# Second block's experts: two slabs loaded ahead instead of four, x kept in SBUF, the last norm taken into the pass by tiles

## What is computed

```python
xf = _rms_norm(h, norm_ffn_w[l]) * (1.0 + scale_f) + shift_f
h = h + gate_f * _hierarchical_moe(xf, w_group[l], b_group[l], w_router[l], b_router[l], w_gate[l], w_up[l], w_down[l])
...
return _rms_norm(h, norm_out_w)
```

## Time and profile before

| | us |
|---|---|
| median of three runs | 3667.17 |
| profiled execution | 3666.75 |
| span of its instructions | 3664.9 |
| TensorE busy in the span | 3198.9 (87%) |
| VectorE busy | 1487.8 (41%) |
| ScalarE busy | 989.3 (27%) |
| GpSimd busy | 46.5 (1%) |

### The profile page before, as it was taken

One profiled execution on the slowest core, in us unless ns is written; L12 is line 12 of the kernel. 1 busy time (PEld: TensorE's weight loads), 2 busy tenths in 40 slices (PEclk: granted clock), 3 DMA queues, 4 the chain that ended last, 5 costly groups with the idle time before them and its releaser, 6 DMA issues. The chain is left out here.

```text
span 3664.9 us, 54483 instructions
## 1 busy us (share of the span) xinstructions
PE 3198.9 (87%) x23420; PEld 1778.7 (49%) x23420; DVE 1487.8 (41%) x3058; ACT 989.3 (27%) x1956; POOL 46.5 (1%) x65
## 2 busy tenths in 40 slices
PE   7889998899889999879995978887989899884996
PEld 3566666666765555444443323334455454541332
DVE  2666667766645685630004101002333424332122
ACT  2343433434313555620002000003224232310001
POOL 0000000000000000000000000000000000000000
PEclk9999999999879999889997999998999999986998
DMA  4122221122231222251135999982301111027998
GB/s 172 52 66 64 65 82 59 61 64 63 64 104 49 69 83 84 84 170 67 60 130 232 421 421 421 421 359 104 118 36 72 46 72 46 0 109 312 413 417 330
DMA packets 119456, 555.31 MB, mean 152 GB/s; under 512 B 32320, under 2 KB 35120, under 8 KB 83632
## 3 DMA queue, kind: packets, MB, share of 16 engines
q1 hardware_dynamic: 113072, 532.95, 38.0%
q0 software_dynamic: 3456, 12.58, 0.9%
q10 hardware_dynamic: 2688, 6.29, 0.4%
HBM read 518.03 MB, written 33.74 MB: 151 GB/s over the span
## 5 line engine op out<-in xcount | busy, mean ns | idle before, releaser
L2332 PE MATMUL mh_ps<-mh_w_ahead,xmT 128*128 128x512 f32 x768 | 336.5, 593 | 0.0
L2067 PE MATMUL ex_ps<-ex_ring,ex_xs 128*64 128x512 f32 x896 | 247.3, 643 | 51.1 <-DMA ex_ring<-expert_slabs_in 43.9
L493 PE MATMUL rw_ps<-hT,rw_w 128*128 128x512 f32 (+1 forms) x640 | 259.0, 535 | 6.1 <-PEq L63 5.8
L2332 PEld LDWEIGHTS mh_ps<-mh_w_ahead,xmT 128*128 128x128 f32 x768 | 144.7, 190 | 167.2 <-issue 165.2
L2067 PEld LDWEIGHTS ex_ps<-ex_ring,ex_xs 128*64 128x64 f32 x896 | 82.6, 148 | 205.6 <-issue 205.6
L1258 PE MATMUL sg_ps<-hTp,sg_w 128*128 128x512 f32 x384 | 170.3, 597 | 0.0
L493 PEld LDWEIGHTS rw_ps<-hT,rw_w 128*128 128x128 f32 x640 | 113.0, 192 | 89.7 <-issue 80.0
L2316 PE MATMUL mh_ps<-xmT,mh_w_ahead 128*128 128x512 f32 x256 | 125.2, 623 | 14.9 <-PEq L63 8.6
L2151 DVE TENSOR_TENSOR ex_hid<-ex_hid,ex_ps 128x512 f32<-128x512 f32 x16 | 11.0, 688 | 288.7 <-PE ex_ps L2067 288.7
L1782 PE MATMUL se_ps<-se_w,se_mT 128*128 128x512 f32 x256 | 113.6, 601 | 8.0 <-DMA se_w<-w_out_in 8.0
L1258 PEld LDWEIGHTS sg_ps<-hTp,sg_w 128*128 128x128 f32 x384 | 73.8, 193 | 91.0 <-issue 90.9
(11 more groups left out here) (602 smaller groups left out, 5349.9 us busy)
## 6 DMA issues: line engine op xcount, KB each, us to landing
ex_ring<-expert_slabs_in SPq DMA_DIRECT2D x148, 1024.0 KB, 26.9
ge_ring<-expert_slabs_in SPq DMA_DIRECT2D x52, 2048.0 KB, 11.7
mh_w_ahead<-head_slabs_in SPq DMA_DIRECT2D x16, 2048.0 KB, 7.9
rw_mod_w<-mod_w_in SPq DMA_DIRECT2D x64, 384.0 KB, 4.0
ex_first<-expert_slabs_in SPq DMA_DIRECT2D x22, 1024.0 KB, 26.3
rw_mod_w<-ada_in SPq DMA_DIRECT2D x64, 256.0 KB, 3.3
sg_kern<-cum_dram SPq DMA_DIRECT2D x64, 256.0 KB, 3.3
ex_ring<-expert_slabs_in SPq DMA_DIRECT2D x7, 2048.0 KB, 13.6
```

Source lines behind the costliest of these rows:

```text
L493: mm = pe.matmul(where[j, part], w[:, k, P * j:P * j + P], tokens, start=k == 0, stop=k == KC - 1)
L2067: mm = pe.matmul(ps[halves[j], bank, :], src[:, k, halves[j]], home(g + j)[0][:, k, :], start=k == 0, stop=k == KC - 1)
L2332: mm = pe.matmul(ps[:, 4 + t, :], xmT[:, k, P * t:P * t + P], w[:, slot, k, :], start=k == 0, stop=k == KC - 1)
```

## The change

1. `settle` takes `x_keep` and, in its third use, `x_out=None`: the sum stays in the SBUF tensor x4, the four stores to x3 are not made. The loads of gate, orow and gate_q are issued at the end of this stage's load list, and counted by a semaphore `landed.rows` that `route` waits for.
2. `route` loads two slabs ahead instead of four, and no x and no rows.
3. In `grouped_experts` SP loads slabs 2 to 5 of pair 0 behind the first rows and quarters. TensorE starts pair 0 after the turn of rows alone; the turn of quarters comes after the first rows product, and both quarter products of pair 0 come after the second rows product.
4. After pair 7 only slabs 0 and 1 of pair 0 are loaded again instead of 0 to 3. Of the last four quarter stores two are issued by SP.
5. `last_residual` is gone: in the pass, each tile's mean, root, reciprocal and product follow its adds, and SP stores it. The products are written to the memory of ge_xs and ge_xsq. A Sqrt of one column is issued ahead of the first tile.

```diff
-                for t in range(NTT):
+                for t in range(NTT if x_out is not None else 0):
                     sp.wait_ge(s.summed, H * t + H)
                     sp.dma_start(x_out[tile(t), :], x[:, t, :]).then_inc(s.x_stored, 16)
...
-        with stage(nc) as (s, block, _):
+        landed, rows = before
+        with stage(nc, landed.all) as (s, block, _):
             @block.sync
             def _(sp):
                 for dst, src in ahead:
                     sp.dma_start(dst, src).then_inc(s.ahead_in, 16)
+                sp.wait_ge(landed.rows, rows)
                 sp.wait_ge(s.ahead_in, 16 * len(ahead))
...
+        normed = lambda t: (xs, xsq)[t // 2][:, t % 2, :, :].rearrange("p k n -> p (k n)")
...
                     load_rows(0)
                     load_quarters(0)
-                    load_slab(0, 4)
-                    load_slab(0, 5)
+                    for n in range(2, 6):
+                        load_slab(0, n)
                     load_rows(1)
-                    for i in range(NP):
-                        nxt = (i + 1) % NP
-                        if 1 <= i and i + 1 < NP:
+                    for i in range(NP - 1):
+                        if i:
                             load_rows(i + 1)
-                        if i % 2 == 1 and i + 1 < NP:
+                        if i % 2 == 1:
                             load_quarters((i + 1) // 2)
                         for n in range(4):
                             sp.wait_ge(s.up_used, 2 * i + n // 2 + 1)
-                            load_slab(nxt, n)
-                        if i + 1 < NP:
-                            sp.wait_ge(s.down_used, i + 1)
-                            load_slab(nxt, 4)
-                            load_slab(nxt, 5)
-                    for n in range(6):
+                            load_slab(i + 1, n)
+                        sp.wait_ge(s.down_used, i + 1)
+                        load_slab(i + 1, 4)
+                        load_slab(i + 1, 5)
+                    sp.wait_ge(s.up_used, 2 * NP - 1)
+                    load_slab(0, 0)
+                    load_slab(0, 1)
+                    sp.wait_ge(s.yeq_kept, NP)
+                    for h in range(2):
+                        sp.dma_start(quarter_rows(NP - 1, 1, h), yeq[quarter[2 + h], :]).then_inc(s.yeq_out, 16)
+                    for t in range(NTT):
+                        sp.wait_ge(s.normed, t + 1)
+                        sp.dma_start(x_out[tile(t), :], normed(t)).then_inc(s.x_stored, 16)
+                    sp.wait_ge(s.x_stored, 16 * NTT)
+                    for n in range(2):
                         sp.wait_ge(slab_in[n], 16 * NP)
...
                     turn_rows(0)
-                    turn_quarters(0)
                     for i in range(NP):
                         last = i + 1 == NP
-                        pe.wait_ge(s.xs_kept, turns_before(i + 1, i // 2 + 1))
+                        pe.wait_ge(s.xs_kept, turns_before(i + 1, i // 2 + 1) if i else 1)
                         for n in range(2):
                             for b in range(2):
-                                if i:
-                                    pe.wait_ge(slab_in[2 * n + b], 16 * i)
+                                if n:
+                                    pe.wait_ge(slab_in[2 + b], 16 * i + 16)
+                                elif i:
+                                    pe.wait_ge(slab_in[b], 16 * i)
...
-                            up_quarters(i, n)
+                            if i:
+                                up_quarters(i, n)
+                            elif n == 0:
+                                turn_quarters(0)
+                        if i == 0:
+                            pe.wait_ge(s.xs_kept, 2)
+                            up_quarters(0, 0)
+                            up_quarters(0, 1)
...
-                        for b in range(2):
+                        for b in range(2 if i + 1 < NP else 1):
                             for h in range(2):
...
+                    act.activation(sq[:, 0:1], cst("ones")[:, 0:1], ACT.Sqrt).then_inc(s.squared, 1)
                     for t in range(NTT):
                         act.wait_ge(s.added, t + 1)
-                        if t:
-                            act.wait_ge(s.squared, t)
+                        act.wait_ge(s.squared, t + 1)
                         act.activation(sq[:, :], x[:, t, :], ACT.Square, accum_out=ss[:, t:t + 1]).then_inc(s.squared, 1)
+                        act.wait_ge(s.mean, t + 1)
+                        act.activation(ss[:, t:t + 1], ss[:, t:t + 1], ACT.Sqrt).then_inc(s.root, 1)
...
+                    def scale(t):
+                        dve.wait_ge(s.root, t + 1)
+                        link(dve.reciprocal(ss[:, t:t + 1], ss[:, t:t + 1]))
+                        dve.scalar_tensor_tensor(normed(t), x[:, t, :], ss[:, t:t + 1], orow, ALU.mult, ALU.mult).then_inc(s.normed, 1)
...
                         ins.then_inc(s.added, 1)
+                        if t:
+                            scale(t - 1)
+                        dve.wait_ge(s.squared, t + 2)
+                        dve.tensor_scalar(ss[:, t:t + 1], ss[:, t:t + 1], 1.0 / D, EPS, ALU.mult, ALU.add).then_inc(s.mean, 1)
+                    scale(NTT - 1)
```

More of the change, by code:

```diff
@@ L1958, in _ @@
                 dve.tensor_copy(lg.rearrange("p t n -> p (t n)"), ps[:, 6, 0:NL * NTT])
-def last_residual(nc, ss, orow, x, x_out):
-    NTT = SEQ // P
-    with stage(nc) as (s, block, _):
-        @block.sync
-        def _(sp):
-            for t in range(NTT):
-                sp.wait_ge(s.normed, t + 1)
-                sp.dma_start(x_out[P * t:P * t + P, :], x[:, t, :]).then_inc(s.x_stored, 16)
-            sp.wait_ge(s.x_stored, 16 * NTT)
-        @block.scalar
-        def _(act):
-            act.wait_ge(s.mean, 1)
-            act.activation(ss, ss, ACT.Sqrt).then_inc(s.root, 1)
-        @block.vector
-        def _(dve):
-            link = linker(dve, s.dve_link)
-            dve.tensor_scalar(ss, ss, 1.0 / D, EPS, ALU.mult, ALU.add).then_inc(s.mean, 1)
-            dve.wait_ge(s.root, 1)
-            link(dve.reciprocal(ss, ss))
-            for t in range(NTT):
-                dve.scalar_tensor_tensor(x[:, t, :], x[:, t, :], ss[:, t:t + 1], orow, ALU.mult, ALU.mult).then_inc(s.normed, 1)
 CAP = 2 * SEQ // NE
@@ L2752, in first_of_ties, with route @@
         link(dve.tensor_tensor(hot[:, :, e], hot[:, :, e], a, ALU.is_gt))
-def route(nc, cst, raw, bias, weight, slot, npass, ahead):
+def route(nc, cst, raw, bias, weight, slot, npass, ahead, before):
     NTT, G, E = SEQ // P, 4, 4
@@ L3296, in program @@
                 mixer_heads(nc, masks, xmT, tok, a["head_slabs"], a["gdn_taps"], a["ret_decay"], rope, norm_w[:, :], m, w, xe_dram[0:NE * SLOTS, :])
-            settle(nc, cst, (m, a["w_out2"], None, None), (mod2[0:1, 2 * D:3 * D], None), (col_a, col_sh), x2, x3,
-                   (a["norm_ffn"], part(mod2, 0, 4), part(mod2, 0, 3)), (a["route_w"], 20), wide(20), xn_keep=xn)
+            gate_of = lambda lo, hi, n: mod2[0:1, 5 * D + lo:5 * D + hi].broadcast_to([n, hi - lo])
+            rows = [nc.sbuf_tensor(name, shape, F32, side="right") for name, shape in (("x4", [P, 4, D]), ("gate4", [P, D]), ("gate_q", [P, 512]), ("orow4", [P, D]))]
+            x, gate, gate_q, orow = (keep.enter_context(r) for r in rows)
+            landed = Sems(nc, keep)
+            settle(nc, cst, (m, a["w_out2"], None, None), (mod2[0:1, 2 * D:3 * D], None), (col_a, col_sh), x2, None,
+                   (a["norm_ffn"], part(mod2, 0, 4), part(mod2, 0, 3)), (a["route_w"], 20), wide(20), xn_keep=xn, x_keep=x,
+                   ahead=[(gate[:, :], gate_of(0, D, P), landed.rows), (orow[:, :], a["norm_out"].broadcast_to([P, D]), landed.rows)] +
+                         [(gate_q[32 * n:32 * n + 32, :], gate_of(512 * (n % 2), 512 * (n % 2) + 512, 32), landed.rows) for n in range(4)])
         with ExitStack() as moe:
             sb = lambda name, shape: moe.enter_context(nc.sbuf_tensor(name, shape, F32))
-            x, gate, gate_q, orow, ss = sb("x4", [P, 4, D]), sb("gate4", [P, D]), sb("gate_q", [P, 512]), sb("orow4", [P, D]), sb("ss4", [P, 4])
+            ss = sb("ss4", [P, 4])
             ye_dram = scratch("ye_dram", (NE * SLOTS, D))
@@ L3305, in program @@
             npass = moe.enter_context(nc.sbuf_tensor("npass", [P, 1], mybir.dt.int32))
[L3306 to L3310 removed]
+            route(nc, cst, wide(20), route_b, weight[:, :, :], slot[:, :, :, :], npass[:, :], [(ring[:, n, :], a["expert2_slabs"][n]) for n in range(2)],
+                  (landed, 96))
             grouped_experts(nc, cst, slot[:, :, :, :], weight[:, :, :], npass, (col_a, col_sh), xn, (xe_dram, ye_dram), a["expert2_slabs"], ring,
[L3312 to L3313 removed]
+                            (gate[:, :], gate_q[:, :]), x, ss, orow[:, :], out)
 def kernel(**inputs):
```

24 lines of the change are left out of this document (10 added, 14 removed).

## The result

The changed kernel takes 3643.93 us (3640.17 to 3645.55, four runs) where the kernel before takes 3667.43 beside it (four runs): ratio 0.9935, 95% interval 0.9918 to 0.9952, so 23.5 us faster. The forecast was 3643.6. The profiled execution took 3643.77 us.

A forecast was written before the change was run, and what follows sets the result against it. Routing was taken as bound by its loads, pairs by TensorE with transfers close behind, the tail by vector work and small transfers. Gains 17.5 + 0 + 0 + 3.1 + 0 + 3.0 = 23.6 us gave 3643.6 us, range 3640.5 to 3646 (0.72).

The forecast's parts named there:

- Part 1: Route stage: without two slab loads, x and six row loads, VectorE is late next; gain 17.5 us, bounds 17.0 to 18.0.
- Rival (c): Route stage: the second slab lands as late as the third did, 3.3 us less gain, 3646.9 us; chance 0.04.
- Parts 2 and 3: Row loads moved into settling, x stores dropped: 0, at most 0.5 us lost; scatter with the same eight indirect DMAs: 0.
- Part 4: First pair: first product ahead of the turn of quarters, less clock loss; gain 3.1 us, bounds 1.2 to 3.7.
- Part 5: Steady pairs: refills shift, lead of the next pair's rows shrinks 3.5 us to 1.7; no loss, bounds 0 to 3 us.
- Rival (a): Pairs 1 to 3: lead gone, TensorE waits for rows or slabs, 3 to 6 us together, 3646.6 to 3649.6; chance 0.14.
- no reserve in rate: Steady pairs: each moves 14.15 MB in 34.0 us, 416 GB/s against 417 shown, so transfers have reserve only in lead.
- Rival (d): Seven refilled pairs: transfers set the pace, 4.4 us more each at 368 GB/s, kernel 7.3 us slower; chance 0.02.
- Part 6: End of the pass: split quarter stores 1.3 us, norm stage gone 1.7 us; gain 3.0 us, bounds 1.2 to 4.3.
- two take 1.4 us, so the gathers start 1.3 us earlier: End of the pass: ScalarE issues two quarter stores instead of four, which took 2.77 us; gain 1.3 us.
- The Sqrt table load: End of the pass: put where ScalarE idles 23.76 us, cost 0; coming back at each tile, 5.1 us in all.
- Rival (b): Tail: GpSimd's gathers and VectorE's operations delay each other; two operations per gather cost about 4 us, 3647.6; chance 0.04.

The follow-up runs named there:

- four_ahead: Changed kernel with routing loading four slabs ahead again, and four reloaded at the end of the pass; x and rows stay out of routing: 3653.17 us.
- x_back: Changed kernel with x stored to memory again by the second settling stage and loaded back in routing behind its two slabs: 3645.27 us.
- after_again: The changed kernel run once more without an edit, for its scatter: 3641.52 us, ratio to the kernel before 0.9923.
- warm_34: Changed kernel plus 34 unused 128x512 products on TensorE ahead of pair 0's turn of rows: 3655.27 us.
- quarters_first: Changed kernel with the turn of quarters made before pair 0's first product again, loads unchanged: 3643.97 us, ratio to the kernel before 0.9931.
- stores_on_act: Changed kernel with all four last quarter stores issued by ScalarE again, still two slabs reloaded: 3641.74 us.
- wrap4: Changed kernel with slabs 0 to 3 of pair 0 reloaded after pair 7 instead of 0 and 1, stores still split: 3642.82 us.
- traffic_1mb: Changed kernel plus one unread 1 MB load per pair in pairs 1 to 6: 3651.00 us.
- traffic_half: Changed kernel plus one unread 0.5 MB load per pair in pairs 1 to 6: 3649.72 us.

## Why the prediction was right, and where its steps were not

**Part 1, route: right.** 17.5 forecast, 17.56 measured; ge_row 17.23 us after the logits where 17.3 was worked out (3310.7 less 3293.39). The reading that SP's wait for the last load held the stage, and that VectorE is next, is shown by four_ahead and x_back. Rival (c) is out: the second slab landed 1.7 us ahead of VectorE's last write, the third load would have been 3.9 us too late (21.08 against 17.2).

**Parts 2 and 3: right,** at nothing. The six row loads were issued from 3235.07 to 3237.84 in the settling stage, which took 80.31 us against 81.12. In the stretch from 3240 to 3260 the DMA share fell from 0.13 to 0.02: what I had read there was the first x store (issued at 3243.39). And the scatter took 15.98 us against 15.97.

**Part 4, first pair: right within its bounds, by up to 0.5 us too high.** 3.1 forecast; 2.60 measured in the first profile, 3.05 in the second. The order is worth 3.9 us where I had 3.6. The clock took more than I allowed: the first product ran 2.60 us over its warm time in after (2.16 in after_again) against 1.34 in before. That is a loss of 0.8 to 1.3 us where the term was 0.5. Out of the bounds of 1.35 to 2.2 for the whole loss I had taken 1.85; it was 2.16 and 2.60. The slabs came in time, as worked out.

**Part 5, pairs: right in the sum, near the edge.** No loss, 245.80 us in both. The lead did shrink, by 4.8 us and not by 3.5: pair 2's rows were issued at 3375.05 and landed 20.2 us later, at 3395.25. The two rows, landing and use:

```profile
DMA to landing us min/median/max: 20.2/20.2/20.2
...
3395.64 1.04 PE L2937 MATMUL ge_ps<-consts,ge_xg 128*128 128x128 f32 x8
```

So 0.4 us were left where I had 1.7; in eight other profiles with this order it is 0.2 to 0.4 (1.0 in warm_34, where pair 0 began 13 us later behind the same loads). Rival (a) missed by no more than that: that nothing stalled was partly luck. quarters_first, with the old order, has 4.5 us there, so it is the later release of the first slabs that spends the lead. What I had wrong is "no reserve in rate": with a limit of 425 against a demand of 416 GB/s a lag shrinks, and the lead grows again, 1.2 us for pair 3 (3409.41 plus 19.5, wanted at 3430.14), 2.2 for pair 4 and 3.2 for pair 7 (3545.40 plus 17.5, wanted at 3566.12). Rival (d) needed 368 GB/s; the transfers carry 425. The 377 GB/s of the earlier trace rows, its one row in favour, has a DMA share of 0.95 beside it and holds the moment between the second refill and the third, as the prediction's part 5 had said itself. The figure of the Trainium skill that I had set beside it, about 358 GB/s for a core ("DMA: Bandwidth & Descriptors", section "Specifications"), is the rate of a memory stack shared out over two cores; here one core runs, and this loop shows 417 to 426.

**Part 6, tail: too low, by 1.6 us.** 3.0 forecast, 4.64 measured (2.07 - 0.27 + 3.13 - 0.29) in the first profile, a little beyond the bound of 4.3. Two terms were off.
- The step "two take 1.4 us, so the gathers start 1.3 us earlier" gave the split a gain of 1.3. It measured 0.3 to 0.7. The gain ahead of the gathers was 2.07 because of the two slabs that are no longer loaded again, to which I had given nothing: I had asked only what is queued on SP's queue, not how long a small store takes among transfers of others. The sum was nearer than its reason.
- The norm was put at 1.7 and is worth 2.9 to 3.3. The working had 19.85 us from the first add to the last product's end, and it takes 18.42. Three tiles take 0.30 us less each for reciprocal, product and mean (1.46 against 6.1/4 + 0.23 = 1.76), and the last tile's handoff takes 0.53 us from the end of the product ahead (3634.95 + 1.29) to the start of the last one, at 3636.77, where 0.75 stood beside a mean and a reciprocal of their own: 0.7 less. Against that the late row took 0.81 us and not 0.4. I had added busy times of small operations that overlap their neighbours.

The Sqrt table load was hidden, as worked out (3612.76, behind the last quarter stores), and did not come back. Rival (b) has its mechanism and no price that shows, instead of 4 us. Its reading that the earlier trace rows shows a third of the lock (0.44 us) was wrong: a gather waits for the whole rest of the add, which was partly over when the gather began.

**The sum.** By seams the change is worth 24.8 us in the first profile, 1.2 more than forecast. The scatter ahead of the logits took 1.9 of it back, and the time outside of the span was 1.67 us instead of 1.85. The median's 0.3 us of difference to the forecast is closer than the steps deserve: their errors were +0.1, -0.5 and +1.6 us, and the total of one kernel moves by more than these (3641.52 us in the second set). So the closeness is luck; the parts' sum, 24.8 against 23.6, is the fair measure. Why the stretch ahead of the third settling stage varies by up to 12 us between profiles was not looked into.

## What to carry to other kernels

A stage that preloads for the next one ends with its last load: count the bytes in the queue, keep what is needed first, and let the rest ride behind the first consumer; here each 2 MB past the second slab cost some 4 us. Where transfers and TensorE run at the same pace, a DMA share of 1.01 doesn't say how much is left: compare the GB/s with what the loop asks for, or add a known load and see what it costs. Ahead of a small transfer on the critical path, look also at the large ones under way on any queue, and of small VectorE operations in a row take the distance of their starts, not their busy times.

## What the hardware showed that I had not expected

- TensorE's clock fell within an idle time of 2.81 us, right after more than 20 us of unbroken work at 2.4 GHz: granted 0.91 over the 3 us of the gap and 0.53 over the next three. In another kernel it held through 2.13 us of idle time after work of some 15 us. The same start of pair 0, with the same work of TensorE ahead, gave first products of 8.61 to 9.69 us in ten profiles.
- One product of 128x512 with a 128x128 float32 operand is two matmuls of 0.43 us.
- A store of 64 KB landed 1.6 to 1.9 us after its issue (after, stores_on_act), and 2.2 to 3.7 us after it in the kernels that had two more loads of 2 MB under way (before, wrap4); its issue on ScalarE took longer too (four in 2.77 us against 1.75).
- GpSimd's gathers take 0.93 to 0.98 us to issue alone. One that begins during an add of VectorE takes longer by the rest of that add less some 0.12 us, up to 1.99 us in all (traffic_1mb), in each such gather of all profiles; no add took longer for it than 1.28 to 1.35 us.
- The DMA engines carried 425 to 426 GB/s over 160 us for one core (after, traffic_half, traffic_1mb).
